# Groups A and B of a streaming encoder step: PSUM banks dealt out anew, and the rows turned one step later

## The reference

```python
def attend(q, k, v, bias, mask, sink=None):
    ...
    s = jnp.einsum('bqhgd,bkhd->bhgqk', qg, k).astype(F32) * (d ** -0.5)
    s = s.reshape(b, hq, tq, -1) + bias
    s = jnp.where(mask, s, NEG_INF)
    ...
        p = jax.nn.softmax(s, axis=-1)
    ...
    o = jnp.einsum('bhgqk,bkhd->bqhgd', p, v)

# A: bias = rel_bias_a(a_table, ...), keys of the own chunk of 64 and of 8 chunks back
# B: F = cumsum(log forget gate); bias = F[query] - F[key], key position <= query position
```

## Time and profile before

| | us |
|---|---|
| median of 3 runs | 4377.17 |
| lowest and highest | 4371.15, 4381.04 |
| the profiled execution, its own time | 4374.29 |
| its span, first to last instruction | 4372.5 |
| mean granted TensorE clock, share of full speed | 0.945 |
| PE busy in the span | 3836.7 (88%) |
| DVE busy | 2250.8 (51%) |
| ACT busy | 1593.5 (36%) |

### The profile page before, as it was taken

How to read it: one execution, slowest core, us unless ns; L and a number is a source line. 1 busy time by engine, 2 the same in 40 slices (tenths; PEclk the granted TensorE clock), 3 DMA queues, 4 the chain that set the end, 5 groups by cost and what they waited for, 6 DMA issues and landing times. The chain is left out here.

```text
span 4372.5 us, 51419 instructions
## 1 busy us (share of the span) xinstructions
PE 3836.7 (88%) x18129; PEld 2643.7 (60%) x18129; DVE 2250.8 (51%) x4858; ACT 1593.5 (36%) x2424; POOL 682.4 (16%) x408
## 2 busy tenths in 40 slices
PE   5999999968888999996998779889877699999698
PEld 3789988966666566564874544443344455555376
DVE  7211111137776444443230199999678876666332
ACT  3100001104444334333320189995345333333333
POOL 3100000011212111111430000000032632211133
PEclk8999999989999999998999899999979799999899
DMA  5221122133334223212431211111243210100243
GB/s 184 69 73 67 63 73 81 65 84 82 92 91 99 63 60 74 64 36 91 160 126 63 63 38 57 56 58 48 80 104 94 61 39 23 25 21 3 97 154 125
DMA packets 222512, 328.51 MB, mean 75 GB/s; under 512 B 22224, under 2 KB 129032, under 8 KB 220896
## 3 DMA queue, kind: packets, MB, share of 16 engines
q1 hardware_dynamic: 173280, 236.21, 18.9%
q10 hardware_dynamic: 43776, 72.50, 4.5%
q0 software_dynamic: 5216, 16.70, 1.8%
HBM read 214.35 MB, written 110.99 MB: 74 GB/s over the span
## 5 line engine op out<-in xcount | busy, mean ns | idle before, releaser
L1017 PE MATMUL attAB_p_o<-attAB_pt,attAB_v 128*65 128x512 f32 (+3 forms) x1120 | 441.3, 492 | 3.0 <-ACT attAB_pt L1064 3.0
L1104 DVE TENSOR_REDUCE attAB_mx<-attAB_p_s 128x1 f32<-128x512 f32 (+2 forms) x360 | 210.7, 608 | 313.1 <-PE attAB_p_s L952 200.6
L497 DVE COPY ab_stage<-ab_pA 128x256 f32<-128x256 f32 (+1 forms) x108 | 56.5, 523 | 603.5 <-PE ab_pA L466 579.4
L2360 DVE TENSOR_SCALAR_CACHE_REDUCE cd_junk<-score,cd_thr 128x512 bf16<-128x512 f32 (+8 forms) x288 | 350.3, 1274 | 1.4 <-DVE cd_thr L2377 0.3
L2398 ACT ACTIVATE cd_gate<-score,cd_thr 128x384 bf16<-128x384 f32 (+2 forms) x192 | 322.3, 1679 | 23.3 <-DVE cd_thr L2377 16.1
L994 PE MATMUL attAB_p_t<-attAB_q_a,attAB_k_a 128*128 128x512 f32 (+3 forms) x560 | 314.0, 564 | 0.0
L464 PE MATMUL ab_pA<-ab_W_hi,h_hi 128*128 128x256 f32 x1088 | 309.0, 284 | 3.3 <-PE ab_pA L466 3.2
L465 PE MATMUL ab_pA<-ab_W_lo,h_hi 128*128 128x256 f32 x1088 | 307.9, 283 | 0.0
L466 PE MATMUL ab_pA<-ab_W_hi,h_lo 128*128 128x256 f32 x1088 | 307.8, 283 | 0.0
L495 ACT ACTIVATE ab_stage<-ab_pA 128x256 f32<-128x256 f32 (+1 forms) x108 | 50.1, 464 | 700.3 <-PE ab_pA L466 669.5
L1625 PE MATMUL attD_p_o<-attD_pt,attD_v 128*65 128x512 f32 x548 | 287.6, 606 | 0.0
(11 more groups left out here) (343 smaller groups left out, 8809.4 us busy)
## 6 DMA issues: line engine op xcount, KB each, us to landing
attAB_raw<-t_k SPq DMA_DIRECT2D x32, 640.0 KB, 7.3
attAB_raw<-t_q SPq DMA_DIRECT2D x32, 640.0 KB, 9.7
t_qg<-cd_stage SPq DMA_DIRECT2D x74, 256.0 KB, 2.0
ab_W_raw<-in_w_ab SPq DMA_DIRECT2D x17, 1024.0 KB, 5.8
mix_o<-t_o SPq DMA_DIRECT2D x34, 512.0 KB, 4.3
t_q<-ab_stage ACTq DMA_DIRECT2D x40, 256.0 KB, 2.0
t_k<-ab_stage ACTq DMA_DIRECT2D x40, 256.0 KB, 2.0
norm_x<-in_x ACTq DMA_DIRECT2D x17, 512.0 KB, 3.6
```

The source lines that it names most:

```text
L1017: done = nc.tensor.matmul(p_o[u % 2][0:VW, i0 * P:(i0 + n) * P], left, pt[c % NPT][:, at * P:(at + n) * P], start=(c == plan.chunks_of[u][ ...
L2360: nc.vector.tensor_scalar(junk[nth % 2][:, 0:widths[n]], sc[n][:], T[:, n:n + 1], None, ALU.is_ge, ALU.add, accum_out=cnt[s % 2][:, n:n + ...
```

## The change

The eight banks are dealt out anew: `p_s` gets three, `p_t` two. `bank_free` then asks for what was written at g - 3, and `scores(c)` waits for the reader of chunk c - 2 instead of chunk c - 3. A unit's row moves from step `due[u] + 1` to `due[u] + 2`, and within a step from behind the maxima to ahead of them, on PE and in the numbering of the bank uses. ACT's copy of the row, which follows `plan.rows_at`, moves one step with it.

```diff
-            self.rows_at[due[u] + 1].append(u)
+            self.rows_at[due[u] + 2].append(u)
...
-            order += self.max_at[c] + [("row", u) for u in self.rows_at[c]]
+            order += [("row", u) for u in self.rows_at[c]] + self.max_at[c]
...
-        p_s = [ps(f"p_s{k}") for k in pair]
-        p_t = [ps(f"p_t{k}") for k in range(3)]
+        p_s = [ps(f"p_s{k}") for k in range(3)]
+        p_t = [ps(f"p_t{k}") for k in pair]
...
-            if g >= 2:
-                last = plan.order[g - 2]
+            if g >= 3:
+                last = plan.order[g - 3]
...
-                    if c >= 3:
-                        pe.wait_ge(exped if kind_of(c - 3) == "B" else t_biased, c - 2)
+                    if c >= 2:
+                        pe.wait_ge(exped if kind_of(c - 2) == "B" else t_biased, c - 1)
...
                     if c + 2 < NT:
                         scores(c + 2)
+                    for u in plan.rows_at[c]:
+                        shift_row(u)
                     for m in plan.max_at[c]:
                         maximum(m)
-                    for u in plan.rows_at[c]:
-                        shift_row(u)
```

More of the change, by code:

```diff
@@ L949, in maximum @@
                     for x, (at, hi, lo, k0, w) in enumerate(parts):
-                        out, ks = p_s[g % 2][:, at * P:(at + w) * P], slice(k0 * P, (k0 + w) * P)
+                        out, ks = p_s[g % 3][:, at * P:(at + w) * P], slice(k0 * P, (k0 + w) * P)
                         nc.tensor.matmul(out, q_a[j][:, rows], hi[:, ks], start=(x == 0), stop=False)
@@ L954, in maximum @@
                     if diagonal:
-                        done = nc.tensor.matmul(p_s[g % 2][:, (n - 1) * P:n * P], identb[:], tri[:], start=False, stop=True)
+                        done = nc.tensor.matmul(p_s[g % 3][:, (n - 1) * P:n * P], identb[:], tri[:], start=False, stop=True)
                     done.then_inc(scored, 1)
@@ L963, in shift_row @@
                     for i in range(len(blocks)):
-                        done = nc.tensor.matmul(p_s[g % 2][0:FORGET, i * P:(i + 1) * P], shift[u % 2][:, i, :], ident_r[:],
+                        done = nc.tensor.matmul(p_s[g % 3][0:FORGET, i * P:(i + 1) * P], shift[u % 2][:, i, :], ident_r[:],
                                                 start=(i == 0), stop=(i + 1 == len(blocks)))
@@ L991, in scores @@
                         cols = slice((blocks[0] + i0) * P, (blocks[0] + i0 + n) * P)
-                        out = p_t[c % 3][:, at * P:(at + n) * P]
+                        out = p_t[c % 2][:, at * P:(at + n) * P]
                         diagonal = kinds[h] == "B" and t == (blocks[i0] if blocks[0] < LAST else n_cache[h])
@@ L1062, in exponent @@
                         act.wait_ge(valued, c - NPT + 1)
-                    src = p_t[c % 3] if kind_of(c) == "B" else s_t[c % NST]
+                    src = p_t[c % 2] if kind_of(c) == "B" else s_t[c % NST]
                     nc.scalar.activation(pt[c % NPT][:, 0:w], src[:, 0:w], ACT.Exp).then_inc(exped, 1)
@@ L1071, in keep_row @@
                     nc.scalar.activation(q_b[h % 2][SHIFT:FORGET, blocks[0] * P:blocks[0] * P + w],
-                                         p_s[g % 2][SHIFT:FORGET, 0:w], ACT.Copy).then_inc(row_kept, 1)
+                                         p_s[g % 3][SHIFT:FORGET, 0:w], ACT.Copy).then_inc(row_kept, 1)
                 def keep(u):
@@ L1100, in reduce @@
                     dve.wait_ge(scored, m + 1)
-                    out, src = mx[u % 2][:, i, nth:nth + 1], p_s[g % 2][:, 0:n * P]
+                    out, src = mx[u % 2][:, i, nth:nth + 1], p_s[g % 3][:, 0:n * P]
                     h, blocks = plan.units[u]
```

8 lines of the change are left out of this document (4 added, 4 removed).

## The result

The changed kernel takes 4282.19 us, the median of runs from 4278.92 to 4283.86. The kernel before took 4374.45 beside it. The ratio is 0.9783, with an interval of 0.9771 to 0.9795, so it is faster by 92 us. The forecast was 4310 us with a range from 4284: the sign was right, and the gain was over a third larger than the 67 us worked out.

What follows compares the result with a forecast made beforehand. The prediction took PE to bound attention, so its idle time counts: A 41 us plus B 26 us, sum 67, from the profiled 4374.29 us gives 4307, adjusted by 2.9 us to the median: 4310 us, range 4284 to 4345.

Steps and rivals of the forecast that it cites:

- PE's waits for `p_s`: In A and B, PE's entries for `p_s` banks fall from 61 us to a few; the `shift` entry goes.
- B, 26 us: Gain in group B: 28.9 us of waits gone, less 3 us for the lost `p_t` bank.
- The 3 us set aside for the `p_t` bank: In B, scores waiting for ACT's exponential behind a row: 8 us at most over 40 units, 3 taken.
- the term 28.9: In B, all of PE's recorded waits, 28.9 us, are for `p_s` banks and go with the third bank.
- A, 41 us: Gain in group A: 22.5 us from long waits, 18 from short ones, rounded up for the first head's start.
- 3.2 us for the two long waits: Gain per A head at the waits behind POOL's key split and DVE's query split; ends 2.2 and 6.2.
- The short waits at dense maxima: In A, 18 us of many short PE waits, gone because the third `p_s` bank lets PE go further ahead.
- The slow stretch behind the second wait: In A, PE at 1.2 GHz behind the query-split wait, assumed to stay; one slow stretch costs 1.59 us.
- A new entry of about 2 us per head: In A, scores waiting for DVE's bias addition once a head, about 2 us, as the wait moves from the row.
- A's waits: Rival: DVE sets A's pace, so PE's waits move to the scores; about 4340 us; chance 0.14.
- The slower rival: Scores wait through row, copy, exponential in all 80 units, 1.28 us each, 102 us: 4412 us; chance 0.06.
- No gain: Rival: each wait returns at the next dependence, in A and B: 4377 us; chance 0.06.

Runs made afterwards that it cites:

- e3_two_and_two: Kernel before with the row one step on and ahead of the maxima, two `p_s` and two `p_t` banks, one bank idle: 4356.70 us.
- e4_behind: Changed kernel with the row kept in its new step but behind that step's maxima: 4319.45 us.
- e9_halves: Changed kernel with DVE's cast and subtraction replaced by reductions, and in A the query split's two instructions two steps apart: 4254.41 us.
- e5_longer_split: Changed kernel with the first instruction of DVE's query split done three times in the A heads: 4325.95 us.
- e1_banks: Changed kernel with its new banks, but the rows at their old place, step due + 1 and behind the maxima: 4334.57 us.
- e2_row: Kernel before with its old banks, but the row one step on and ahead of the maxima: 4354.49 us.
- e6_cast: Changed kernel with DVE's cast of the negated maximum replaced by a second reduction: 4279.83 us.
- e10_old_banks: Kernel before, old banks and rows, with cast and subtraction as reductions and the query split's two instructions apart in A: 4338.03 us.

## Why the prediction was right in direction and short in size

**PE's waits for `p_s`: right.** They fell from 61 us to a few, `shift` is gone from the list but for one wait of 0.7 us, and no wait in B is longer than 0.4 us. ACT's waits at L1071 shrank from 338 to 209 us. All of this is as forecast.

**B, 26 us: right in mechanism, 4 short.** Measured 30.2. The 3 us set aside for the `p_t` bank were about right: at the same clock e3_two_and_two puts some 4 us on it. Why this term is small was argued from where the maxima stand, and e4_behind bears that out: without maxima behind the row it is 23 us more. One argument of that step was faulty, though: I let a short wait hide behind a record of values that overlaps the next scores. It hides in the list, not in time, as the table under e9_halves showed for A. The 4 us lie in the term 28.9, which took the list for the time: between the borders of the first table the list fell from 28.1 to 1.8 us, by 26.3, and the time by 30.2. The step with the second long wait, for one, fell by 1.90 us a head with 1.62 to 1.64 on record; the rest was not followed.

**A, 41 us: the step that failed.** Measured 62.9. The 22 us that are missing came in two parts.

First, the borders. The forecast took the seven heads in the stretch of the earlier trace rows, 1020 to 1372 us, and added half a us for the start of the first. By the timeline, A gained 6.8 us ahead of 1020, where the kernel before has a long wait of 2.19 us and a slow stretch, and 1.3 behind 1372. So some 7.6 us were left out by the borders of the window.

Second, the size of a head's gain, in the two terms of the table under e9_halves. The term that I named as the weakest, 3.2 us for the two long waits, measured (8.62 + 9.76) - (6.09 + 7.74) = 4.55. The short waits at dense maxima, taken from the list as 18 / 7 = 2.6 (which has a fifth entry of 0.9 us in all that I left out), measured 31.83 - 28.53 = 3.3. Together that is 7.86 instead of 5.8, or 14 us in seven heads: 9.5 from the long waits, 5 from the short ones. Why the short ones gave more than their list was not followed.

What failed in the first of these is one sentence: "The slow stretch behind the second wait I leave in, since PE still stands there." PE does stand there, but for 1.34 us instead of 2.20, and behind that the clock stays at 2.4 GHz. The heads of the kernel before show what this is worth, since not each of them has each slow stretch. The one of the six without a slow stretch behind the second wait takes 8.87 us for those three steps, the other five 9.74 to 10.31, so a slow stretch there costs 0.9 to 1.4 us (0.9 to 1.1 without the 10.31, which is the head that has none at the first place). At the first place it is 7.31 without and 8.79 to 8.93 with, or 1.5 to 1.6, as the prediction had it. Both gone makes about 2 us of the 4.55. e5_longer_split gives the counter-proof: made 4.1 us, the same wait brings a slow stretch in every head, and at 1.6 us, in e4_behind, in six of eight. In the third head the forecast had 3.7 against an upper end of 6.2; measured are (8.93 + 9.78) - (6.09 + 7.73) = 4.9.

**A new entry of about 2 us per head: half right.** The sum is 0.71 + 1.34 = 2.05 us, at the forecast place and one more. That it came in two pieces was not foreseen: the forecast had no wait left at the first place, where the scores now wait for the addition behind the held cast. The clock after both is at its full level.

**The rivals.** A's waits did not move in full: A lost 62.9 us. The slower rival, the chain of row, copy, exponential and scores, was priced rightly per link (1.74 us in e1_banks), but it needs the row behind its maxima: there it costs 18.1 us of recorded waits in B, far from 102, since a wait there is 0.48 us on record and not 1.28 (0.61 in time, by e4_behind), 38 units of B have one, and in A there is none. "No gain" fell. The Trainium skill, "TensorE: Matmul & The Clock Gate", section "HAM oscillation", reports that doubled PSUM buffers gave no further gain in its kernel; by that the time would have been 4377, and the measurement, 4282, decides otherwise. In B, though, e1_banks is just such a case: banks alone moved it by 1.1 us.

**Ahead and behind: as assumed.** The two stretches outside the attention changed by -4.4 and +2.1 us; the first is about its scatter.

## What to carry to other kernels

A bank more and an order that lets the engine use it belong together: here, in B, each alone bought nothing (what the row alone won in waits, slow stretches took back) and both bought 30 us, so when a bank is taken from one use, look first at which chain then ends last, and move the head of that chain ahead of the work that can cover it. Price a wait together with the slow clock that follows it: when a wait shortens, ask whether the slow stretch behind it goes too, for that was about a quarter of what an A head gained here. And count the heads, not the window: a stretch cut out for reading leaves out its ends. When two versions differ by little, compare heads at the same clock: e3_two_and_two and e2_row seemed equal because one had fewer slow stretches.

## What the runs showed of the hardware

- A DVE cast of 128x4 elements (kernel after) and a DVE subtraction with two SBUF inputs (e6_cast) that meet POOL's 4.83 us split are held until it has ended: 2.7 to 3.2 us each instead of 0.17, 14 times in the one and 15 in the other, which makes most of the 54 us and the means of 710 and 704 ns above. The reductions that do the same work are not held (152 to 163 ns).
- PE's clock after a wait in A: still at 2.4 GHz behind waits of up to 1.4 us in the kernel after; at 1.2 GHz for 3.4 us behind a wait of 2.0 us before, though not behind one of 1.96 us a head later; at 1.2 GHz for 6.8 us behind waits of 4.1 us in e5_longer_split. The length of the wait alone doesn't decide it: waits of 1.6 us in e4_behind have a slow stretch behind them in six heads of eight, waits of 1.7 to 1.8 us in e1_banks in three of seven, and its first head has 6.8 us at 1.2 GHz behind a wait of 1.33 us.
- A wait of PE is recorded shorter than it is behind a matmul whose record overlaps the next one's: 0.56 us behind the values here, by which the step with 1.34 us on record was 1.91 us too long.
- A slow stretch of 3.41 us costs 1.65 us in B (e2_row), 0.9 to 1.6 in A (before); one of 6.8 us costs 2.5 (e5_longer_split).
- Open: before, B has waits of 1.8 and 1.6 us once a head and no slow stretch; e2_row and e10_old_banks have waits of 1.6 us in B and a slow stretch of 3.41 us in five of its heads. The runs don't tell what makes the difference.
